# Attention and feed-forward in one block, attention tiles released one by one, and a norm placed one chunk later

## The reference

```python
xn  = rmsnorm(x, g_attn_pre)
h   = xn @ w_in                      # latent attention (MLA) and window attention (SWA) inputs
A   = mla(...)                       # 8 heads, block-causal, softmax over all earlier keys
B   = swa(...)                       # window of 128, sinks, relative bias
x   = x + rmsnorm(concat(A, B) @ w_out, g_attn_post)
u   = rmsnorm(x, g_ffn_pre) @ w_up   # 1024 -> 2 * 2816
c   = causal depthwise conv of width 3 over u, plus bias
x   = x + rmsnorm((gelu(c_gate) * c_val) @ w_down, g_ffn_post)
```

## Time and profile before

| | |
|---|---|
| median of three runs | 2811.14 us |
| the profiled execution's own time | 2805.43 us |
| its span, first to last instruction | 2803.6 us |
| mean granted TensorE clock | 0.981 |
| input projection and attention | 0 to about 1002 us |
| feed-forward stage, first matmul | 1014.67 us |
| PE busy over the span | 2675.9 us, 95% |

### The profile page before, as it was taken

One profiled execution on the slowest core, in us unless ns is written; L12 is line 12 of the kernel. 1 busy time (PEld: TensorE's weight loads), 2 busy tenths in 40 slices (PEclk: granted clock), 3 DMA queues, 4 the chain that ended last, 5 costly groups with the idle time before them and its releaser, 6 DMA issues.

```text
span 2803.6 us, 44995 instructions
## 1 busy us (share of the span) xinstructions
PE 2675.9 (95%) x13603; PEld 2441.0 (87%) x13603; DVE 1911.1 (68%) x2793; ACT 1427.5 (51%) x3042; POOL 477.9 (17%) x400
## 2 busy tenths in 40 slices
PE   8999978899999977999999999999999999999997
PEld 7898945677777777999999999999999999999997
DVE  6877667787888827777468755687546875468743
ACT  4444257577666744554345443454434544356532
POOL 0111041244434433000200012000120002200001
PEclk9999989899999989999999999999999999999999
DMA  7656655444455242334334433335333353334432
GB/s 219 213 207 217 202 164 157 89 83 75 85 89 92 56 147 83 110 116 142 112 101 138 161 117 105 102 128 171 117 110 103 121 177 117 111 103 128 130 118 88
DMA packets 181775, 357.73 MB, mean 128 GB/s; under 512 B 50692, under 2 KB 119780, under 8 KB 180324
## 3 DMA queue, kind: packets, MB, share of 16 engines
q1 hardware_dynamic: 181636, 356.00, 43.4%
HBM read 301.28 MB, written 55.43 MB: 127 GB/s over the span
## 4 chain that ended last, share of the span: by engine, by line
PE 56%; DVE 3%; ACT 1%; DMA 1%; issue 1%; POOL 1%; SPq 0%; ACTq 0%; DVEq 0%; POOLq 0%
PE mf_acc L2187 56%; DVE mix_w_lo L2348 1%; DMA room<-in_w_up 1%; ACT mix_w_hi L2241 1%; POOL mf_ss L2143 1%; PE mf_st L2225 0%; DMA room<-in_w_out 0%; DVE mf_x L2366 0%; DVE mf_x L2371 0%; DVE mf_rstd L2383 0%; DVE mf_xn L2399 0%; DVE mf_y L2453 0%; DVE mf_y L2461 0%; ACT mf_sq L2264 0%; ACT mf_sq L2298 0%
## 5 line engine op out<-in xcount | busy, mean ns | idle before, releaser
L2348 DVE TENSOR_TENSOR mix_w_lo<-room,mix_w_hi 128x1024 fp32r<-128x1024 f32 (+1 forms) x338 | 471.2, 1394 | 559.6 <-ACT mix_w_hi L2241 558.9
L2187 PE MATMUL mf_acc<-mix_a_hi,mix_w_hi 128*128 128x424 f32 (+1 forms) x2016 | 722.4, 358 | 32.6 <-ACTq L2244 12.2
L2187 PE MATMUL mf_acc<-mix_a_lo,mix_w_hi 128*128 128x424 f32 (+1 forms) x2016 | 716.1, 355 | 0.0
L2187 PE MATMUL mf_acc<-mix_a_hi,mix_w_lo 128*128 128x424 f32 (+1 forms) x2016 | 716.0, 355 | 0.0
L2241 ACT ACTIVATE mix_w_hi<-room 128x1024 fp32r<-128x1024 f32 (+1 forms) x338 | 383.0, 1133 | 520.4 <-PE mf_acc L2187 488.9
L2187 PEld LDWEIGHTS mf_acc<-mix_a_hi,mix_w_hi 128*128 128x128 f32 x2016 | 380.8, 189 | 48.5 <-issue 17.2
L2187 PEld LDWEIGHTS mf_acc<-mix_a_hi,mix_w_lo 128*128 128x128 f32 x2016 | 381.5, 189 | 10.5
L2187 PEld LDWEIGHTS mf_acc<-mix_a_lo,mix_w_hi 128*128 128x128 f32 x2016 | 381.0, 189 | 8.7 <-issue 0.7
L2187 PE MATMUL mf_acc<-mf_h_hi,mix_w_hi 128*128 128x424 f32 (+1 forms) x944 | 338.9, 359 | 6.8 <-DVE mix_w_lo L2348 3.8
L2187 PE MATMUL mf_acc<-mf_h_hi,mix_w_lo 128*128 128x424 f32 (+1 forms) x944 | 335.0, 355 | 0.0
L2187 PE MATMUL mf_acc<-mf_h_lo,mix_w_hi 128*128 128x424 f32 (+1 forms) x944 | 334.6, 354 | 0.0
(11 more groups left out here) (204 smaller groups left out, 4119.6 us busy)
## 6 DMA issues: line engine op xcount, KB each, us to landing
room<-in_w_up SPq DMA_DIRECT2D x220, 512.0 KB, 3.6
room<-in_w_down SPq DMA_DIRECT2D x80, 704.0 KB, 4.1
pi_w_raw<-in_w_in SPq DMA_DIRECT2D x49, 512.0 KB, 5.8
room<-in_w_out SPq DMA_DIRECT2D x40, 512.0 KB, 3.6
la_rec_all<-inv_scr SPq DMA_DIRECT2D x32, 256.0 KB
ahead_k<-kn_scr SPq DMA_DIRECT2D x28, 280.0 KB, 5.3
ahead_q<-qn_scr SPq DMA_DIRECT2D x28, 264.0 KB, 5.1
room<-in_x SPq DMA_DIRECT2D x4, 1696.0 KB, 11.5
```

The lines of the kernel that those rows point to most:

```text
L2187: mm = pe.matmul(acc[:, t_bank[0], 0:n], w[:, g, k], x[:, k, 0:n], start=(first and k == 0 and m == 0), stop=(last and k == count - 1 and ...
L2348: dve.tensor_tensor(w_lo[:, g, 0:count], w_raw[:, g, 0:count], w_hi[:, g, 0:count].bitcast(F32), ALU.subtract).then_inc(w_split, 1)
```

## The change

It does six things.

- `attention` no longer opens a block. It returns five functions, which `mix_and_ffn` calls at the head of its own streams; SBUF and PSUM rooms of attention are given back as before, semaphores are kept. POOL's `begin` (constants) moves into the last head's `tail`, after a wait for the last value tile and before the last unit's multiply.
- The weights of chunks 2 and 3 are loaded in the last head at s = 20; `look` of the first pair is skipped by SP. PE's wait `evacuated` is left out for its first two tiles.
- The load of x for block 0 moves from `begin` to `load_second`, behind `y`, and `load_second` moves from after pair 0 to after pair 1. Its semaphore is now `const_in`.
- The hook `att` stands before `look`, and each of tiles 0 to 6 waits only until PE has finished with that tile in the last up chunk (`a_free`); tile 7 waits for the end of the chunk as before.
- In `down_projection` the second `norm` and `invert` move from (2, 0) to (2, 1), one chunk later, and `xn` 0 to 7 stand at (2, 1), (2, 2), (2, 3), (3, 0) (two of them), (3, 1), (3, 2), (3, 3).
- `h_hi` and `h_lo` are allocated last, and `la_prob` before `la_raw`.

```diff
@@ latent_attention, sync, step
+            if not more and s == 20:
+                for g in range(2):
+                    sp.wait_ge(mix["w_split"], g + 1)
+                    sp.dma_start(mix["w_raw"][:, g, 0:KD], d["w_out"][2 + g]).then_inc(mix["w_in"][g], 16)
@@ latent_attention, gpsimd, tail
             norm(LAST, 1, len(ORDER) - 2)
+            pool.wait_ge(pv_done, 2 * NKT * (HEADS // 2))
+            mix_begin(pool)
             norm(LAST, 1, len(ORDER) - 1)
@@ attention
-        block = ctx.enter_context(nc.Block())
-        @block.sync
-        def _(sp):
...
+    def sync(sp):
+        first_row, rest = la["sync"](sp)
+        wa["sync"](sp, first_row)
+        rest()
...
+    return {"sync": sync, "gpsimd": gpsimd, "tensor": tensor, "scalar": scalar, "vector": vector}
@@ mix_and_ffn, walk, up_projection
-                        call("look", B.chunk + 2 * j, g, *nxt)
                         if hook == "att" and g == 1 and B.next and not B.early:
                             for k in range(KD):
                                 call("att", B.next, k, B.chunk + UP_C)
+                        call("look", B.chunk + 2 * j, g, *nxt)
@@ mix_and_ffn, walk, down_projection
+            XN_AT = {(2, 1): (0,), (2, 2): (1,), (2, 3): (2,), (3, 0): (3, 4), (3, 1): (5,), (3, 2): (6,), (3, 3): (7,)}
-                        if e == 0 and N and i % 2 == 0:
+                        if N and (i, e) in ((0, 0), (2, 1)):
                             call("norm", 0, B.norm + i // 2, N.n, B.square + KD + (12 if i else 0))
...
-                        if N and i >= 2:
-                            call("xn", N, 4 * (i - 2) + e)
+                        for k in XN_AT.get((i, e), ()) if N else ():
+                            call("xn", N, k)
@@ mix_and_ffn, walk, opening
-                if i == 0:
+                if i == 1:
                     call("load_second")
@@ mix_and_ffn, sync
+            attend["sync"](sp)
             def begin():
                 sp.dma_start(eps_col[:], d["eps"]).then_inc(const_in, 16)
                 sp.dma_start(gains[:], d["gains"]).then_inc(const_in, 16)
-                sp.dma_start(x1[:, 0:KD], d["x"][:, :, 0:TB]).then_inc(x_in, 16)
             def load_second():
                 load_att(TB, TB)
+                sp.dma_start(x1[:, 0:KD], d["x"][:, :, 0:TB]).then_inc(const_in, 16)
...
             def look(cp, g, kind, idx):
+                if isinstance(cp, int) and cp == 0:
+                    return
                 sp.wait_ge(w_split, cp + g + 1)
@@ mix_and_ffn, tensor
-                if first:
+                if first and not (isinstance(t, int) and t < 2):
                     pe.wait_ge(evacuated, t + 1)
...
+                    if frees and k < count - 1:
+                        mm.then_inc(a_free, 1)
@@ mix_and_ffn, scalar
                 if k == 0:
                     act.wait_ge(att_in, 16 * B.b)
+                if k < KD - 1:
+                    act.wait_ge(a_free, (KD - 1) * (B.b - 2) + k + 1)
+                else:
                     act.wait_ge(chunk_done, c)
```

More of the change, by code:

```diff
@@ L1218, in latent_own, with latent_attention @@
             sb("la_rec", [LA_Q4, 4, LA_CE]))
[L1221 removed]
+def latent_attention(nc, d, ahead, mix, ctx, rooms, ps, wa, own):
     def sb(name, shape, dt=F32):
[L1228 removed]
+        return rooms.enter_context(nc.sbuf_tensor(name, shape, dt))
     def sem(name):
@@ L1794, in latent_attention, with attention, gpsimd, tensor @@
             "scalar": scalar, "vector": vector}
[L1797 to L1807, removed]
-        block = ctx.enter_context(nc.Block())
-        @block.sync
-        def _(sp):
[L1812 to L1839, removed]
+def attention(nc, d, ahead, early, mix, ctx, rooms):
+    ps = rooms.enter_context(nc.psum_tensor("at_ps", [P, 8, 512], F32))
+    own = latent_own(nc, rooms)
+    with ExitStack() as first:
+        wa = window_attention(nc, d, ahead, early, ctx, first, ps)
+    la = latent_attention(nc, d, ahead, mix, ctx, rooms, ps, wa, own)
+    def sync(sp):
+        first_row, rest = la["sync"](sp)
+        wa["sync"](sp, first_row)
+        rest()
+    def gpsimd(pool, mix_begin):
+        la["fills"](pool)
+        wa["rows"](pool)
+        wa["gpsimd"](pool, la["first_values"])
+        la["gpsimd"](pool, mix_begin)
+    def tensor(pe):
+        wa["tensor"](pe, lambda eng: la["tensor"](eng, True))
+        la["tensor"](pe, False)
+    def scalar(act):
+        wa["scalar"](act)
+        la["scalar"](act)
+    def vector(dve):
+        wa["vector"](dve, lambda eng: la["vector"](eng, True))
+        la["vector"](dve, False)
+    return {"sync": sync, "gpsimd": gpsimd, "tensor": tensor, "scalar": scalar, "vector": vector}
+def mix_and_ffn(nc, d, mix, attend):
     with ExitStack() as ctx:
@@ L2114, in load_next @@
                 sp.dma_start(x1[:, bass.ds(B.next.par * KD, KD), 0:B.next.n],
-                             d["x"][:, :, bass.ds(B.next.col, B.next.n)]).then_inc(x_in, 16)
+                             d["x"][:, :, bass.ds(B.next.col, B.next.n)]).then_inc(const_in, 16)
             def end(B):
@@ L2136, in begin @@
                 pool.sem_inc(sq_added, 2)
+            attend["gpsimd"](pool, lambda eng: begin())
             def add_square(kind, slot, sqi, n, first, norm):
@@ L2177, in _, with chunk @@
         def _(pe):
-            def chunk(g, c, t, rhs_hi, rhs_lo, n, count, first, last, wait_k=None):
+            attend["tensor"](pe)
+            def chunk(g, c, t, rhs_hi, rhs_lo, n, count, first, last, wait_k=None, frees=False):
                 pe.wait_ge(w_split, c + 1)
-                if first:
+                if first and not (isinstance(t, int) and t < 2):
                     pe.wait_ge(evacuated, t + 1)
@@ L2208, in ready @@
                     pe.wait_ge(xn_split, KD * B.b + k + 1)
-                chunk(g, c, t, a_hi, a_lo, B.n, KD, True, True, ready if isinstance(j, int) and j == 0 and g == 0 else None)
+                chunk(g, c, t, a_hi, a_lo, B.n, KD, True, True, ready if isinstance(j, int) and j == 0 and g == 0 else None,
+                      isinstance(j, int) and j == KF - 1 and g == 1 and B.next and not B.early)
             def down_mm(B, i, dd, half, c, t):
@@ L2502, in encoder_layer @@
         with ExitStack() as inner:
-            ahead = {"ident": early["ident"], "in": inner.enter_context(nc.semaphore("ahead_in")),
-                     "v_in": inner.enter_context(nc.semaphore("ahead_v_in")),
-                     "head_in": [inner.enter_context(nc.semaphore(f"ahead_head_in{g}")) for g in range(2)]}
+            ahead = {"ident": early["ident"], "in": ctx.enter_context(nc.semaphore("ahead_in")),
+                     "v_in": ctx.enter_context(nc.semaphore("ahead_v_in")),
+                     "head_in": [ctx.enter_context(nc.semaphore(f"ahead_head_in{g}")) for g in range(2)]}
             for name, shape, dt in (("q", [P, 2, 2, TOK], F32R), ("k", [P, 2, 2, KEYS], F32R),
@@ L2508, in encoder_layer @@
                 ahead[name] = inner.enter_context(nc.sbuf_tensor(f"ahead_{name}", shape, dt))
-            attention(nc, d, ahead, early, mix)
-        mix_and_ffn(nc, d, mix)
+            att = attention(nc, d, ahead, early, mix, ctx, inner)
+        mix_and_ffn(nc, d, mix, att)
 def constants():
```

22 lines of the change are left out of this document (11 added, 11 removed).

## The result

The changed kernel takes 2782.83 us (median of three runs, 2777.58 to 2785.48); the kernel before takes 2811.14. The ratio is 0.9891 with an interval of 0.9874 to 0.9909: 28.3 us won, where 22.0 were forecast. The profiled execution took 2777.58 us, its span is 2775.8 us and its mean granted clock 0.985.

The account below looks back on a forecast made before the run. PE, busy for 95% of the span, was taken as the bound, so only its idle time and slow spells could be won: 13.9 + 3.3 + 4.8 = 22.0 us off the 2811.1 median gives 2789.1 us, range 2780 to 2799.

Parts of the forecast that it names:

- Opening: From attention's end through chunks 0 to 7: 18.1 us, less 0.3 at chunk 4, 3.1 at chunk 6, 0.8 slow clock: 13.9 gained.
- Second half of the opening at nothing: Chunks 8 to 15: stalls from DVE's residual work and POOL's sums move with chunk 7's end, so no gain.
- The half spell after chunk 6: After chunk 6's stall PE's clock may drop; a slow spell costs about 1.6 us, half charged: 0.8 us.
- Norm: Four places in the down projections: PE's waits for POOL's sum vanish one chunk later, 4.8 us gained; about 4 us cover left.
- Hook: Three places after the last up chunk: 2.92 us wait mostly handed on; 0.65 us gained each plus one slow spell's 1.4: 3.3.
- the loads cost nothing there: Two weight loads added late in attention, at s = 20: bounds 0 and +0.5 us, taken as 0.
- All covers hold: Rival: chunk 6 is not late and the hook gains all its wait; 33 us saved, 2778 us, chance 0.10.
- 2785 with only chunk 6 in time: Case where only chunk 6's weights arrive in time: 26 us saved, 2785 us, inside the forecast's range.
- The loads cost 2.6 us, not 8: Rival: conv_w's issue, x and y delay chunks 6 and 7 by 8 us; 14 us saved, 2797 us, chance 0.17.
- The meeting is gone: Rival: PE still waits on attention's last store, so only hook and norm gain 8 us; 2803 us, chance 0.04.
- the clock did not stay at the lower level: Rival: without the pause PE stays at 1.2 GHz through the opening's 16 chunks, losing 61 us; 2850 us, chance 0.02.

Follow-up runs that it names:

- Experiment 5: Changed kernel with block 0's x, conv_w, conv_b and the convolution state loaded one chunk pair later; 2783.37 us, ratio 0.9897 to the kernel before.
- experiment 1: Kernel before with only the second norm and xn placed one chunk later; 2803.7 us against 2809.87, ratio 0.9975.
- experiment 3: Changed kernel with only the hook put back (look first, all attention tiles behind the last up chunk's end); 2792.8 us, ratio 0.9941 to the kernel before.
- experiment 4: Changed kernel with a_lo still ahead of look, but all tiles waiting for the last up chunk's end; 2782.12 us, ratio 0.9906 to the kernel before.
- experiment 2: Changed kernel with hook and norm put back as before, leaving the opening's changes alone; 2797.78 us against 2809.87 for the kernel before, ratio 0.9958.
- experiment 9: Changed kernel with block 0's x, the last channel pair's product and the next block's x all moved later; 2775.54 us, ratio 0.9882 to the kernel before.

## Why the prediction was right, and where its sum was not

The forecast was 2789.1 us within 2780 to 2799; measured were 2782.83 and, in the five later runs, 2785.69 (25.3 us won by the medians, 24.2 by the ratio). The mechanism was the one forecast at every place; the clock behind the hook was charged too low.

- **Opening: right.** Forecast 13.9, measured 13.81 us; that they agree to 0.1 us is luck, as the terms miss by up to 0.8 us and cancel. PE goes straight on, at a granted clock of 1.00. Chunk 4 waits 0.73 us in place of 0.3: its load was issued 13.0 us after attention's end, not 12.3, as POOL's multiply came 0.5 us later against that end than before (8.5 in place of 8.0). Chunk 6 waits 2.62 in place of 3.1. Experiment 5 shows its cause, the loads ahead of the weights. The rule of the Trainium skill (DMA: Bandwidth & Descriptors, Queues, rings and completion order), by which each DMA engine consumes the descriptors of a ring in order, spoke against this step of the change, and the trace agrees: `y`, x and weights landed in order of issue, the last after 8.29 us.
- **Second half of the opening at nothing: right** within 0.4 us (52.69 us in place of 52.32, the slow spell behind its longest wait being longer). The waits of 1.47, 1.62, 0.55, 1.64 and 4.88 us stand where 1.50, 1.62, 0.59, 1.61 and 4.96 stood.
- **The half spell after chunk 6: 0.8 charged**, one of seven profiles shows one. The changed kernel's own two profiles have none.
- **Norm: right.** 4.8 forecast, 5.3 in the pair of profiles and 5.9 in experiment 1. Nothing behind it became late, so the cover was enough; whether it is the estimated 4 us no run shows.
- **Hook: the mechanism right, the term mis-sized.** The step that failed is "3 x 0.65 + 1.4 = 3.3 us". The three small waits were 0.81, under 0.15 and 0.97 us against 0.85, 0.3 and 1.2, and in the pair of profiles the hook gave 5.75 - 1.7 = 4.05 us, near the forecast. But the kernel before in that pair seems not to be typical. The 1.4 counts one slow spell after three waits; over the four profiles with the old hook it is 10 of 12, so two or three spells of about 1.5 us. With three, the term is 3 x 0.65 + 3 x 1.5 = 6.5, and experiments 3 and 4, less the 3 us of chance at the loads, give 7 to 8. I took a saving from one execution and subtracted it from a median, having written that this execution lay 5.7 us below that median; the two spells that it did not have would be 3 of those 5.7 us, if the median execution had them, of which there is no profile. This was to be asked: what is missing from the quick execution that the usual one has?
- **Not in the sum:** 1.7 us of shorter waits at the next-block loads, and 2.2 us in attention. I count neither to the change. Attention ended at 1000.25 us in one profile of the changed kernel and at 1005.44 in the other, and between 1002.77 and 1008.45 in the experiments. Its last 500 matmuls, beside which the two added loads are issued, took 104.1 us before and after, so the loads cost nothing there, as forecast; in the other profiles with these loads they took 104.0 to 104.7.

The rivals fell. "All covers hold" (2778), and 2785 with only chunk 6 in time, came near the measured time, but not by their mechanism: chunk 6 was late and the hook kept part of its wait. The time alone would not have told these from the forecast. The loads cost 2.6 us, not 8. The meeting is gone, and the clock did not stay at the lower level when PE no longer rested: it is 1.00 from 1000 to 1078 us, and falls there during the wait of 4.9 us that the kernel before has too.

## What to carry to other kernels

A step's place in an engine's order can be worth more than its handshake: here moving eight subtractions ahead of one weight split gave 7 to 8 us over three places, signalling each tile singly under 1 us. A wait should be priced with what the clock does behind it, and how often it does so can't be read from one profile of three waits. And where two big loads are issued just ahead of weights that are needed, the big one that is wanted last belongs behind them.

## What the runs showed of the hardware that I had not expected

- The granted clock after a wait is not certain. After the hook's waits of 2.91 to 3.00 us, 10 of 12 showed a slow spell; after chunk 6's waits of 2.5 to 2.6 us, 1 of 7. Waits of some 2 us were seldom followed by one, but were: chunk 2's 1.94 us before the change and experiment 3's 2.09 at a next-block load did, the 2.03 of the kernel before did not, and of the stops of 1.6 to 2.1 us at the start of block 2's up projection, one in each of the twelve profiles, the one of experiment 2 (2.10) did. The twelve waits of 3.1 to 3.2 us in block 0's first up chunks, the twelve of 4.9 in the opening and the long ones (9.55 and 12.2 us) all did. A single spell cost 1.4 to 1.6 us whether it followed a wait of 2.5 us or of 9.55; behind the two pauses of 12.2 us it cost 1.9 us (kernel before) and 2.8 us (experiment 1).
- The issue of a small DMA (`conv_w`) held SP for 5.57 and 4.18 us with two 1.7 MB loads outstanding just ahead of it, and for 0.65 and 0.72 us (experiments 5 and 9) when they were spaced out.
- One and the same kernel reached the end of attention 5.2 us apart in two executions, more than the norm or the hook's term in the sum. Single profiles are best compared from a common point on: from there its two profiles agreed within 1.0 us.
